# Matrix memory in 16 steps of two heads and attention in 16 steps with deeper buffers, in a one-core block kernel

## The reference, cut to what matters

```
b_t    = cumsum(log_f);   g_s = log_i_s - b_s;   m_t = running max of g
S[s,t] = exp(g_s - m_t) * (k_s . q_t)     for s <= t (forward) or s >= t (backward)
num_t  = sum_s S[s,t] * v_s
den_t  = sum_s S[s,t]
h_t    = num_t / max(|den_t|, exp(-(b_t + m_t)))
```

## Time and profile before

| | |
|---|---|
| median of three runs | 1709.56 us (1706.21 to 1710.54) |
| the profiled execution | 1704.78 us, of which the span of instructions 1703.0 us |
| TensorE busy | 92% of the span, 6827 matmuls |
| VectorE, ScalarE, GpSimd busy | 52%, 36%, 22% |
| mean granted TensorE clock | 0.966 of full |
| chain of work that ended last | of little use here: it names only 6% of the span |

### The profile page before, as it was taken

One profiled execution on the slowest core, in us unless ns is written; L12 is line 12 of the kernel. 1 busy time (PEld: TensorE's weight loads), 2 busy tenths in 40 slices (PEclk: granted clock), 3 DMA queues, 4 the chain that ended last, 5 costly groups with the idle time before them and its releaser, 6 DMA issues. The chain is left out here.

```text
span 1703.0 us, 18596 instructions
## 1 busy us (share of the span) xinstructions
PE 1566.9 (92%) x6827; PEld 1181.6 (69%) x6827; DVE 892.6 (52%) x1229; ACT 609.8 (36%) x912; POOL 372.2 (22%) x468
## 2 busy tenths in 40 slices
PE   4899999999899999677899999999889999989967
PEld 3788888888685555234688888888667778766646
DVE  4776337333633343655543434433446446799974
ACT  3422222222433232334343312222432134677644
POOL 3011000000000000002000678730201200499910
PEclk9899999999999999769999999999999999999988
DMA  9788426332231111001233242354123223222201
GB/s 344 221 267 281 155 80 198 99 102 64 79 105 32 37 38 50 25 0 39 80 99 99 90 145 88 111 186 167 50 81 97 83 62 108 70 77 82 76 25 50
DMA packets 203731, 176.34 MB, mean 104 GB/s; under 512 B 6907, under 2 KB 183367, under 8 KB 203142
## 3 DMA queue, kind: packets, MB, share of 16 engines
q1 hardware_dynamic: 188438, 121.87, 24.3%
q0 software_dynamic: 14064, 51.34, 8.6%
q10 hardware_dynamic: 1152, 2.10, 0.3%
HBM read 166.90 MB, written 8.39 MB: 103 GB/s over the span
## 5 line engine op out<-in xcount | busy, mean ns | idle before, releaser
L1944 PE MATMUL ps<-h_hi,w_hi 128*128 128x512 f32 x1224 | 491.2, 401 | 29.2 <-DVE h_lo L1261 14.3
L1946 PE MATMUL ps<-h_hi,w_lo 128*128 128x512 f32 x1224 | 480.7, 393 | 0.0
L1945 PE MATMUL ps<-h_lo,w_hi 128*128 128x512 f32 x1224 | 480.3, 392 | 0.0
L1221 DVE TENSOR_TENSOR w_lo<-w_stage,w_hi 128x1024 fp32r<-128x1024 f32 x225 | 294.3, 1321 | 232.1 <-ACT w_hi L775 229.7
L1944 PEld LDWEIGHTS ps<-h_hi,w_hi 128*128 128x128 f32 x1224 | 232.0, 190 | 104.9 <-issue 52.6
L775 ACT ACTIVATE w_hi<-w_stage 128x1024 fp32r<-128x1024 f32 x225 | 230.8, 1048 | 195.7 <-PE ps L1946 187.5
L1946 PEld LDWEIGHTS ps<-h_hi,w_lo 128*128 128x128 f32 x1224 | 231.7, 189 | 49.7
L1945 PEld LDWEIGHTS ps<-h_lo,w_hi 128*128 128x128 f32 x1224 | 232.2, 190 | 47.1 <-issue 1.2
L1944 PE MATMUL ps<-a_hi,w_hi 128*128 128x512 f32 x544 | 213.8, 393 | 13.1 <-DVE a_lo L1880 9.4
L1946 PE MATMUL ps<-a_hi,w_lo 128*128 128x512 f32 x544 | 212.3, 390 | 0.0
L1945 PE MATMUL ps<-a_lo,w_hi 128*128 128x512 f32 x544 | 212.2, 390 | 0.0
(11 more groups left out here) (416 smaller groups left out, 1582.4 us busy)
## 6 DMA issues: line engine op xcount, KB each, us to landing
w_stage<-in_w_gu SPq DMA_DIRECT2D x88, 512.0 KB, 4.3
ada_w<-in_w_ada POOLq DMA_DIRECT2D x72, 512.0 KB, 6.4
w_stage<-in_w_down SPq DMA_DIRECT2D x44, 512.0 KB, 3.7
w_stage<-in_w_in SPq DMA_DIRECT2D x24, 512.0 KB, 3.8
w_stage<-in_odd_w_in SPq DMA_DIRECT2D x24, 512.0 KB, 3.7
w_stage<-in_even_w_in SPq DMA_DIRECT2D x16, 512.0 KB, 3.9
w_stage<-in_w_out SPq DMA_DIRECT2D x8, 512.0 KB, 3.9
mats<-mats_d POOLq DMA_DIRECT2D x4, 1024.0 KB, 7.3
```

The lines of the kernel that those rows point to most:

```text
L1221: dve.tensor_tensor(w_lo[:, c % RING], w_in[:, c % RING], w_hi[:, c % RING].bitcast(F32), ALU.subtract).then_inc(w_split, 1)
L1944: pe.matmul(bank, w_hi[:, slot, k], rhs_hi, start=start, stop=False, skip_group_check=True)
L1945: pe.matmul(bank, w_hi[:, slot, k], rhs_lo, start=False, stop=False, skip_group_check=True)
L1946: return pe.matmul(bank, w_lo[:, slot, k], rhs_hi, start=False, stop=stop, skip_group_check=True)
```

## The change

It works on `mlstm`, its tails, `attention` and the first two tiles of `project_out`.

- `mlstm` has 16 steps. A step treats two heads (r = 0, 1) of one direction, whose 64-row score products sit at partitions 0 to 63 and 64 to 127 and go to two banks. Projection slices: three before the sums and three after.
- Sums: the weighted scores (`e_m`, now multiplied in place) are the stationary operand, one 128 x 128 block at a time, and `vm`, which has got a column of ones, is the moving operand with 129 columns. The result has positions in partitions, and its last column is the denominator. `strip` is gone.
- Maxima: POOL stores `neg_m` to DRAM and loads each needed row spread over 128 partitions (`bm`, in SBUF). `spread` is gone.
- Tails: DVE forms quotients from PSUM per pair (`quotients`) in place of ACT's copy; the sum of squares is a DVE reduction along the row, scale a DVE product; then PE transposes each head back (`turn_head`) and `head_out` gates it. Head 0 is done within `mlstm`, the others early in the attention.
- Queries and keys are rotated first and normalised last, with the gain put in ACT's copy; `swap` comes ahead of `head_ones`.
- `attention` has 16 steps of a pair of heads. Four buffers for pairs (`e_of`, in the room of mq, mk and vm), scores in four banks, transposes in banks 2 and 5, all copies out of PSUM on ACT, the values after every second step (8 products of 256 columns). Scores of pair 0 are issued in the last step of `mlstm`.
- `ln_count` is kept as one 128 x 896 table of distances and loaded when the last key tile is done. 7 of 8 slices of the first tile of `w_out` are made ahead of the last values, and 7 of the second right after them.

```diff
-MSTEPS = 8 * MH
+MSTEPS = 4 * MH
...
-        vm = put("vm", [P, ST, S])
+        vm = put("vm", [P, ST, MH, P + 1])
...
+            pool.wait_ge(g_chain, 10)
+            pool.dma_start(nm_d, neg_m[:]).then_inc(nm_stored, 16)
+            pool.wait_ge(nm_stored, 16)
+            for d in range(4):
+                upto(pool, e_ready, 8 * (d - 1))
+                for r in range(2):
+                    row = d % 2 * 32 + d // 2 * 2 + r
+                    pool.dma_start(bm[:, d % 2 * 2 + r], nm_d[row:row + 1, :].to_broadcast([P, S])).then_inc(bm_in[d % 2], 16)
+            pool.wait_ge(qk_done, 8)
+            pool.dma_start(ln_count[:], a["ln_count"]).then_inc(lnc_in, 16)
...
+                        upto(act, p_used, 2 * (i - 2) + r + 1)
...
+            def quotients(d):
+                for r in range(2):
...
+                    dve.wait_ge(p_used, 8 * d + 6 + r + 1)
...
+                    for t, b in banks:
+                        ins = dve.scalar_tensor_tensor(den[:, t], b[:, :, P], -1.0, gcol[:, 1, t, row], ALU.mult, ALU.max)
+                    link(ins)
+                    for t, b in banks:
+                        ins = dve.tensor_tensor(den[:, t], den[:, t], b[:, :, P], ALU.max)
+                    link(ins)
+                    link(dve.reciprocal(den, den))
+                    if d % 2 == 0:
+                        for t, b in banks:
+                            ins = dve.tensor_tensor(hm[:, h, t], b[:, :, 0:P],
+                                                    den[:, t].unsqueeze(2).to_broadcast([P, t.stop - t.start, P]), ALU.mult)
+                    else:
...
+                                ins = dve.scalar_tensor_tensor(hm[:, h, k], b[:, k - t.start, 0:P], den[:, k:k + 1], hm[:, h, k],
+                                                               ALU.mult, ALU.add)
...
+                def scores(i):
...
+                    for r in range(2):
+                        part = slice(r * DH, (r + 1) * DH)
+                        upto(pe, p_ready, 2 * (i - 1) + r + 1)
+                        pe.matmul(ps[3 + r][:, a0:a1], mk[part, d // 2, st * P:(st + 1) * P], mq[part, d // 2, a0:a1],
+                                  start=True, stop=True).then_inc(sc_ready, 1)
+                def sums(i):
...
+                    if i % 4 == 0:
+                        upto(pe, num_ready, 2 * d)
+                    for r in range(2):
+                        pe.wait_ge(p_ready, 2 * i + r + 1)
+                        for tt in range(a0 // P, a1 // P):
+                            bank, at = (ps[5 + r], tt * (P + 1)) if tt < 3 else (ps[7], r * (P + 1))
+                            mm = pe.matmul(bank[:, at:at + P + 1], e_m[:, i % 2 * 2 + r, tt * P:(tt + 1) * P],
+                                           vm[:, st, d // 2 * 2 + r], start=(i % 4 == 0 and (tt == 0 or tt == 3 and r == 0)),
+                                           stop=(st == tt), skip_group_check=True)
+                        mm.then_inc(p_used, 1)
...
+                scores(0)
+                for i in range(MSTEPS):
+                    parts_of_tiles(i * PER_STEP)
+                    for m in ends_at(i - 1):
+                        if m < 8:
+                            pe.wait_ge(proj_read, FIRST + m)
+                            upto(pe, qk_rs, 2 * m - 1)
+                            pe.matmul(ps[2][:], swap[:], tmp[:, m % 2], start=True, stop=True).then_inc(qk_rot, 1)
+                        else:
+                            turn_back(m)
...
+                    sums(i)
+                    if i + 1 < MSTEPS:
+                        scores(i + 1)
                     else:
+                        pair_scores(0)
+                    parts_of_tiles(i * PER_STEP + PER_STEP // 2)
...
+                        if m < 8:
+                            pe.wait_ge(rot_read, m + 1)
+                            pe.matmul(ps[2][:], head_ones[:], tmp2[:, m % 2], start=True, stop=True).then_inc(qk_sum, 1)
...
+                for q in range(4 * MH + 3):
+                    if 0 < q < 4 * MH:
+                        pair_scores(q)
+                    if q in (1, 5, 6):
+                        if q == 1:
+                            pe.wait_ge(num_ready, 8)
+                        turn_head({1: 1, 5: 2, 6: 3}[q])
+                    if 2 <= q < 4 * MH + 2:
+                        back(q - 2)
+                    if q == 4 * MH + 1:
+                        pe.wait_ge(s_max, 8 * MH)
+                        part_of_out(0, range(KT - 1))
+                    if q >= 4 and q % 2 == 0:
+                        values((q - 4) // 2)
```

More of the change, by code:

```diff
@@ L165, in constants @@
             "rope_cos": np.tile(cos, (2, 1)), "rope_sin": np.tile(sin, (2, 1)),
-            "swap": swap, "head_ones": heads, "strip": strip, "pick": pick}
+            "swap": swap, "head_ones": heads, "pick": pick}
 def upto(eng, sem, value):
@@ L945, in mlstm @@
                 act.preload_act_table_set("natural_log_exp_and_others")
                 decay(0)
[L947 to L954, removed]
+                for i in range(MSTEPS):
+                    for m in ends_at(i - 2):
@@ L963, in head_part @@
[L963 to L977, removed]
@@ new lines, in mlstm @@
+                    if i % 4 == 2 and i < 12:
+                        diagonals(i // 4 + 1)
+                    if i + 1 < MSTEPS:
+                        weigh(i + 1)
+                    for m in ends_at(i):
+                        lo(0, T_MIX + FIRST + m + 2)
+                    if i in (9, 10):
+                        head_sum(i - 9)
+                    if i in (11, 12):
+                        head_scale(i - 11)
+                    if i == 13:
+                        head_out(0)
@@ new lines, in attention @@
+                    if 1 <= q <= 4 * MH:
+                        s = 2 * q - 2
+                        dve.wait_ge(s_exp, s + 2)
+                        link(dve.reciprocal(mx[:, 3, s:s + 2], mx[:, 2, s:s + 2]))
+                        for r in range(2):
+                            e = e_of[(q - 1) % 4][:, r]
+                            dve.tensor_scalar(e, e, mx[:, 3, s + r:s + r + 1], None, ALU.mult).then_inc(p_norm, 1)
+                    if q in (1, 2):
+                        head_sum(1 + q)
@@ new lines, in parts_of_tiles @@
+                def parts_of_tiles(first):
+                    for j in range(first, first + PER_STEP // 2):
+                        m, k = divmod(j, KT)
+                        n = FIRST + m
+                        if k == 0:
+                            pe.wait_ge(w_split, T_MIX + n + 1)
+                            pe.wait_ge(proj_read, n - 2)
+                        mm = three(ps[n % 2][:], (T_MIX + n) % RING, k, h_hi[:, k], h_lo[:, k], k == 0, k == KT - 1)
+                        if k == KT - 1:
+                            mm.then_inc(w_used, 1)
```

562 lines of the change are left out of this document (262 added, 300 removed).

## The result

The kernel after takes **1602.84 us** (median of four runs, 1601.4 to 1607.28) against 1707.88 us for the kernel before in the same comparison: a ratio of 0.9395, with a 95% interval of 0.9363 to 0.9426. It is faster, by 105 us where 78 were forecast, and lies under the range of 1610 to 1670. The profiled execution took 1601.4 us, its span 1599.7.

What follows compares the result with a forecast made beforehand. PE's work was taken to bound the matrix memory (stage 1), a loop of short waits the attention (stage 2). 1704.8 - 35.7 (stage 1) - 42.1 (stage 2) = 1627.0 us profiled, plus 4.8 gives 1632 us; range 1610 to 1670.

Steps and rivals of the forecast that it cites:

- Strip and spread: Matrix memory: removing the strip products saves 21.1 us of PE time, removing the spread products 4.3 us.
- The steps of the attention: Attention: each step of a pair of heads takes 3.5 us, so 16 steps take 56 us.
- The maxima by DMA at nothing: Matrix memory: sending maxima through DRAM costs nothing because loads are covered; uncovered, 5 to 10 us a time.
- a low clock: Rival, attention: PE's clock stays at 0.50, adding 35 us, for 1667 us; chance 0.15.
- a longer loop: Rival, attention: the loop of waits takes 5 us a step, adding 24 us, for 1656 us; chance 0.13.
- bare loads: Rival, sums: weight loads don't overlap products, 0.43 us a product, adding 10 us, for 1642 us; chance 0.06.
- slower: Rival, both stages: small waits keep the clock at 0.50 throughout, up to 1773 us; chance 0.04.
- I take 0.30, 24 us, so a loss of 3.8 on this item: Matrix memory sums: 80 turned products of 129 columns at 0.30 us each, against 20.2 us for the numerators before.
- Scores in pairs: Matrix memory: paired score products on the two halves of the rows overlap, 11.9 us for 20.2, saving 8.3.
- So 8 us of new waits: Matrix memory: 3 us waiting for quotients, 1 at the start, 4 for one clock fall, against 11.7 us old.
- Once VectorE waits for the root ...: 2: Attention: DVE waits once for the root of heads 2 and 3 behind ACT's copies, 2 us.
- Loss of clock at the start ...: 4: Attention start: PE stands for 2 to 3 us and the clock falls, costing 4 us.

Runs made afterwards that it cites:

- values in halves: The kernel after with each values step of the attention cut into two halves, one ahead of every pair of transposes: 1604.1 us, stage 2 68.1 us.
- scores apart: The kernel after with a projection slice between the two score products of each step, so they can't run together: 1617.3 us, stage 1 128.3 us.
- the kernel with the wait ahead: The kernel after with PE's wait for the quotients ahead of a direction's first three slices instead of behind them, three times: 1615.1 us, stage 1 126.3 us.

## Why the prediction was right in direction and wrong in size

The forecast for a profiled execution was 1627.0 and the measured one 1601.4. 18.4 of the 25.6 us lie in stage 1 (132.9 forecast, 114.5 measured), 6.3 in stage 2 (73.2 and 66.9), 0.9 elsewhere.

**What held.** Each stage was bounded as said: doubling the sums showed stage 1 to be PE's. Strip and spread: 25.4 forecast, 25.3 measured. The steps of the attention: 3.5 us forecast, 3.48 measured, but by luck in part: the forecast took them from a loop of 6.8 us through maxima and normalising, and with values in halves two steps pass in 6.47, so that loop does not bind at 6.8. What binds in the kernel after is the wait of 0.83 us until ScalarE has copied the transposes out of their banks. The first transposes 9.2 us behind the last sums: 8.8. Seven slices of `w_out` and the last values: 7.0 and 6.8. The maxima by DMA at nothing: confirmed. The rivals of a low clock, a longer loop and bare loads all fall, and "slower" with them.

**The steps that failed.**
- "I take 0.30, 24 us, so a loss of 3.8 on this item": the product cost 0.245, 19.6 us in all, so a gain of 0.6 on the 20.2 that I had for the numerators before. I had taken the price of a lone 128-column product, with a switch of kind on either side; in groups of 4 to 16 passes the switch is shared, and the rows of eight and sixteen passes were the nearer ones. 4.4 us.
- "Scores in pairs ... a saving of 8.3": 11.0 at full clock (12.5 less the 1.5 of low clock). I gave the narrow scores the price of narrow numerators (0.74 at 384), where a score product of 384 columns takes 0.84 by itself, in the kernel before and in the one with scores apart. 2.7 us.
- "So 8 us of new waits": 1.25. Only one of the three waits for quotients shows:

```profile
605.22 2.05 PE L2128 MATMUL ps<-vm,e_m 128*128 128x129 f32 x16 [1.25 <-DVE hm L1485]
```

  The other two and the wait at the start that I had added are hidden, and no fall of the clock came. VectorE's quotients were dearer in my count than they are: one head, backward, with four blocks takes 1.04 us for the blocks and some 0.7 for its small instructions, 1.8 for 2.2.

```profile
628.14 1.13 DVE L1491 SCALAR_TENSOR_TENSOR hm<-ps,mx,hm 128x128 f32<-128x128 f32 x4
629.18 0.21 DVE L1477 SCALAR_TENSOR_TENSOR mx<-ps,gcol 128x3 f32<-128x3 f32 x2
```

  With the waits of the stage before, which were 7.1 and not the 5.2 that I had taken from two of them, 8.5 us.
- The slices and the small products with them, which the sum left as they were: 2.9 us less than that. Three slices now run on into the next three, so there are 16 switches of kind fewer, at about 0.2 us each by the kernel with scores apart. This cause was not tested by itself.
- Stage 2: "Once VectorE waits for the root ...: 2" and "Loss of clock at the start ...: 4" were added to 16 steps of 3.5. From the first transposes to the end of the last, 634.80 to 691.07, are 56.3 us where 62 were forecast. The clock did fall there (from 639.0), and this cost nothing; the second fall, which I had not placed, cost 1.7, and without it the stretch takes 54.6. VectorE waited 1.4 us for the root once, but no wait of PE names it. I had laid two allowances on a period that already had room in it. 6 us.

**The common fault** is that nearly every unknown was taken on its dear side, and the low end of the range then corrected only three of them. Bounds from both sides have to be summed on the cheap side too: by the sums at 0.215, scores from their own rows, no new wait and no fall, the same sum would have come to 1627.0 - 7 - 3 - 8 - 6 = 1603 for a profiled execution.

**Where the attention's gain came from** was left open by the sum, and the runs name it: 31.6 us for the tails, 5 for the depth, 4.3 of wait for the table before (a late table costs 2.0 in the new order); what is left, some 8 us, goes with scores in step and a clock of 0.95, and was not split further. The tails were taken out of the kernel before, the depth out of the one after, and the 4.3 are a wait that was read and not removed, so the split is rough.

## What to carry to other kernels

Where TensorE is the bound of a stage, count its passes by kind, from groups of the size that will be issued, and look for small products that belong to another job: spreading a row, summing a column and adding ones cost this kernel 44 us of PE before, and a column of ones, a reduction along the row, a DMA and a few transposes (2.2 us) took their place. Serial tails mixed into a pipeline cost their waits twice, since a stand of some 2 to 4 us can bring the clock down as well. And when only a part of a program changes, cut the trace there: times of stage 1 agreed to 0.1 us where whole runs differed by 9. Look at the clock inside the cut before comparing: one fall more or less was 1.7 us here, as much as the edits under test.

## What was not expected of the hardware

- A fall of the clock is not sure: behind a wait of 2.19 us it held at full, behind 2.94 and 3.77 it fell to 0.50. Behind one and the same wait of 1.89 us of the attention it fell in after's execution and held in the one of the kernel with the wait ahead, 1.7 us apart. A fall cost from nothing (where PE had slack) to 1.7 or 2 us.
- A stationary block of 128 columns for each pass of 129 columns costs no more than the pass: 0.12 us with a new block, 0.111 with the one before loaded again. Products of 512 columns take 0.95 us in two passes, which is 0.12 for 129 columns too.
- Two score products on the two halves of the rows take 0.85 us at 384 columns, and one alone 0.84: the second is free.
- Most of the whole time's spread of 2 to 9 us lies ahead of the mixer's two stages: the first scores started between 510.8 and 517.9 us in twelve profiled executions with the same program up to there.
